# A token-major second MLP product, attention scores from rounded halves, and queries projected in smaller parts

## The reference

```python
s = jnp.einsum('bqhgd,bkhd->bhgqk', q_blk, k, preferred_element_type=jnp.float32) * (HEAD_DIM ** -0.5)
p = jax.nn.softmax(s, axis=-1).astype(v.dtype)
...
x = x + gt1[..., None, :] * branch_merge(attn_x, gla_x, ga, gg, w_br_attn, w_br_gla, w_out)
x = x + gt2[..., None, :] * sq_relu_mlp(modulate(rms_norm_2(x, norm2), sh2, sc2), w_mlp1, w_mlp2)
...
def sq_relu_mlp(h, w1, w2):
    return jnp.square(jax.nn.relu(h @ w1)) @ w2
```

## Time and profile before

| what | value |
|---|---|
| median of three runs | 1803.73 us (1802.23 to 1803.89) |
| the profiled execution, its own time | 1801.4 us |
| its span, from first to last recorded instruction | 1799.6 us |
| TensorE busy | 1737.3 us, 97% of the span |
| VectorE, ScalarE, GpSimd busy | 1020.6, 802.6, 725.2 us |
| granted TensorE clock, mean | 0.998 of full speed |
| HBM traffic | 84 GB/s over the span |

### The profile page before, as it was taken

How to read it: one execution, slowest core, us unless ns; L and a number is a source line. 1 busy time by engine, 2 the same in 40 slices (tenths; PEclk the granted TensorE clock), 3 DMA queues, 4 the chain that set the end, 5 groups by cost and what they waited for, 6 DMA issues and landing times.

```text
span 1799.6 us, 25063 instructions
## 1 busy us (share of the span) xinstructions
PE 1737.3 (97%) x9011; PEld 1399.6 (78%) x9011; DVE 1020.6 (57%) x1560; ACT 802.6 (45%) x1364; POOL 725.2 (40%) x795
## 2 busy tenths in 40 slices
PE   8999999998999899999999999999999999999998
PEld 6777777776777567778878888888888878888887
DVE  6688786677647874456649838766733331212122
ACT  4445454466546664345552254564533342313231
POOL 3645545443543104321114432233244545555563
PEclk9999999999999999999999999999999999999999
DMA  6342422221222001211018721112123323333332
GB/s 209 91 121 89 126 85 82 71 69 37 76 92 76 20 17 50 71 43 29 24 56 277 232 68 42 42 47 59 47 83 94 105 71 101 99 94 93 104 95 94
DMA packets 238798, 152.11 MB, mean 85 GB/s; under 512 B 7997, under 2 KB 223046, under 8 KB 238694
## 3 DMA queue, kind: packets, MB, share of 16 engines
q1 hardware_dynamic: 225758, 125.50, 24.1%
q10 hardware_dynamic: 12936, 25.21, 4.1%
HBM read 148.59 MB, written 2.10 MB: 84 GB/s over the span
## 4 chain that ended last, share of the span: by engine, by line
PE 65%; issue 11%; DVE 8%; POOL 7%; ACT 7%; DMA 1%; POOLq 0%; DVEq 0%; ACTq 0%; SPq 0%
PE ps L657 17%; PE ps L661 17%; PE ps L658 16%; POOL wl L607 7%; PE ps L2176 2%; PE ps L2158 1%; PE ps L1614 1%; PE ps L1646 1%; ACT wh L620 1%; PE ps L2165 1%; PE ps L2645 1%; PE ps L2679 1%; DVE pairs L2917 1%; PE ps L2159 1%; DVE queries L1917 1%
## 5 line engine op out<-in xcount | busy, mean ns | idle before, releaser
L607 POOL TENSOR_TENSOR wl<-raw,wh 128x256 fp32r<-128x256 f32 (+1 forms) x775 | 701.7, 937 | 1014.3 <-ACT wh L620 1014.3
L657 PE MATMUL ps<-ah,wh 128*128 128x512 f32 (+1 forms) x1144 | 461.8, 404 | 12.5 <-ACT gate_u L2718 4.2
L661 PE MATMUL ps<-ah,wl 128*128 128x512 f32 (+1 forms) x1144 | 447.6, 391 | 0.3
L658 PE MATMUL ps<-al,wh 128*128 128x512 f32 (+1 forms) x1144 | 446.3, 390 | 0.0
L620 ACT ACTIVATE wh<-raw 128x1024 fp32r<-128x1024 f32 (+1 forms) x220 | 230.6, 1049 | 305.2 <-PE ps L661 293.3
L657 PEld LDWEIGHTS ps<-ah,wh 128*128 128x128 f32 (+1 forms) x1144 | 214.0, 187 | 68.0 <-issue 11.1
L661 PEld LDWEIGHTS ps<-ah,wl 128*128 128x128 f32 (+1 forms) x1144 | 213.7, 187 | 49.9 <-POOL wl L607 2.1
L658 PEld LDWEIGHTS ps<-al,wh 128*128 128x128 f32 (+1 forms) x1144 | 214.3, 187 | 44.2 <-issue 1.4
L657 PE MATMUL ps<-bh,wh 128*128 128x512 f32 (+1 forms) x588 | 232.8, 396 | 5.7 <-DVE resid L1471 2.6
L661 PE MATMUL ps<-bh,wl 128*128 128x512 f32 (+1 forms) x588 | 230.0, 391 | 1.5 <-POOL wl L607 1.4
L658 PE MATMUL ps<-bl,wh 128*128 128x512 f32 (+1 forms) x588 | 229.1, 390 | 0.0
(11 more groups left out here) (434 smaller groups left out, 2729.2 us busy)
## 6 DMA issues: line engine op xcount, KB each, us to landing
raw<-w_mlp SPq DMA_DIRECT2D x64, 512.0 KB, 3.8
raw<-w_in SPq DMA_DIRECT2D x52, 512.0 KB, 3.7
raw<-ssm_w_in SPq DMA_DIRECT2D x40, 512.0 KB, 3.8
ada_late<-w_ada ACTq DMA_DIRECT2D x16, 1024.0 KB, 6.7
ada_raw<-w_ada ACTq DMA_DIRECT2D x16, 512.0 KB, 3.8
raw<-ssm_w_out SPq DMA_DIRECT2D x16, 512.0 KB, 3.3
raw<-mla_w_in SPq DMA_DIRECT2D x11, 512.0 KB, 3.7
raw<-mla_w_out SPq DMA_DIRECT2D x8, 512.0 KB, 3.5
```

What stands on the lines that cost most here:

```text
L607: nc.gpsimd.tensor_tensor(wl[:, s, part], raw[:, s, part], wh[:, s, part].bitcast(F32), ALU.subtract).then_inc(lo_ready, LOW_PIECES * (par ...
L657: nc.tensor.matmul(dst, w_hi[k], x_hi[k], start=k == 0, stop=False)
L658: nc.tensor.matmul(dst, w_hi[k], x_lo[k], start=False, stop=False)
L661: ins = nc.tensor.matmul(dst, w_lo[k], x_hi[k], start=False, stop=k == n - 1)
```

## The change

Six things at once.

1. The second MLP product is token-major: hidden activations are stationary (128 tokens), 512 columns of the weights move, and 4 token tiles by 2 column halves go to 8 PSUM banks. Each half's results are multiplied by the gate, laid out as rows (`gate_rows`), and added to `o_tok`, which starts as the transposed `resid`. The transposes, 8 groups of 4, move to the front of the MLP; the gate rows are made by 8 matmuls of `ones` by a diagonal matrix. Results are stored in 8 parts instead of 4.
2. The scores of the grouped-query attention are made of three fp32r matmuls of high and low halves, for which ScalarE and VectorE split queries and keys. The key head 1 is scaled later, projections of queries keep a distance of two heads, the sum of squares moves from t = 1 to t = 0.
3. The query projection of the latent attention is spread over all four heads of a quad: 9, 6, 6 and 6 matmuls.
4. The two `modulation` calls are put apart, before units 8 and 9.
5. `stay_busy(2, 9)` before the first scores of the latent attention is new; in front of the MLP `stay_busy(3, 10)` and `stay_busy(3, 16)` become `stay_busy(1, 10)`.
6. ScalarE's second and third `take_q` of a quad come one head later (`Q_TAKEN`).

```diff
-                if g < CTX_BLOCKS // 2:
-                    modulation(2 * g)
-                    modulation(2 * g + 1)
                 for n in range(8, 10):
+                    if g < CTX_BLOCKS // 2:
+                        modulation(2 * g + n - 8)
                     projection("ssm", g, n)
...
             project_q(0, 1)
+            stay_busy(2, 9)
             scores(0)
...
-                if h // QUAD + 1 < QUADS and h % QUAD < 3:
-                    project_q(h // QUAD + 1, h % QUAD)
+                if h // QUAD + 1 < QUADS:
+                    for piece, ks in Q_PARTS[h % QUAD]:
+                        project_q(h // QUAD + 1, piece, ks)
...
+        Q_PARTS = (((0, (0, 1, 2)),), ((1, (0, 1)),), ((1, (2,)), (2, (0,))), ((2, (1, 2)),))
+        Q_TAKEN = (0, None, 1, 2)
...
-                nc.tensor.matmul(bank(b), q, k_feat[:, j // QPK, 0:T], start=True, stop=True)
-                nc.tensor.matmul(bank(b + 1)[:, 0:CTX], q, k_feat[:, j // QPK, T:TA], start=True, stop=True).then_inc(sem("g_scores"), 1)
+                terms = ((q_hi, k_hi), (q_hi, k_lo), (q_lo, k_hi))
+                for cols, dst in ((slice(0, T), bank(b)), (slice(T, TA), bank(b + 1)[:, 0:CTX])):
+                    for k, (q, keys_) in enumerate(terms):
+                        ins_ = nc.tensor.matmul(dst, q[:, j % 2, tile], keys_[:, j // QPK, cols], start=k == 0, stop=k == 2)
...
+            def high_q(j):
+                nc.scalar.activation(q_hi[:, j % 2], p_cos[:], ACT.Copy).then_inc(sem("qk_high"), 1)
+            def low_q(j):
+                nc.vector.tensor_tensor(q_lo[:, j % 2], p_cos[:], q_hi[:, j % 2].bitcast(F32), ALU.subtract).then_inc(sem("qk_low"), 1)
...
-            stay_busy(3, 10)
+            for c in range(DC):
+                ins_ = nc.tensor.matmul(bank(2 + c // 4)[:, c % 4 * P:(c % 4 + 1) * P], ones[:], gate_diag[:, c], start=True, stop=True)
+            for k in range(3):
+                turn_resid(k)
             norm_pe_summed(pe, "norm2", norm_v[:, 1])
-            stay_busy(3, 16)
+            turn_resid(3)
+            turn_resid(4)
+            stay_busy(1, 10)
...
+            def token_major(i, half, q):
+                last = q == DC // OUT_KS - 1
+                for k, t in ([(k, t) for t in range(TT) for k in range(OUT_KS)] if last else [(k, t) for k in range(OUT_KS) for t in range(TT)]):
+                    c, tok, dst = q * OUT_KS + k, slice(t * P, (t + 1) * P), bank(OUT_BANKS[half][t])
+                    nc.tensor.matmul(dst, bh[:, c, tok], vh[:, k], start=c == 0, stop=False)
+                    nc.tensor.matmul(dst, bl[:, c, tok], vh[:, k], start=False, stop=False)
+                    low(k, T)
+                    ins_ = nc.tensor.matmul(dst, bh[:, c, tok], vl[:, k], start=False, stop=c == DC - 1)
...
-                for c in range(DC):
-                    nc.vector.scalar_tensor_tensor(resid[:, c], bank(c % 2), mod[:, 5 * DC + c, 0:1], resid[:, c], ALU.mult,
-                                                   ALU.add).then_inc(acc_free[c % 2], 1)
+                for k in range(2 * TT):
+                    part = nc.vector.tensor_tensor(out_part[k % 2], bank(b), gate_rows[:, cols], ALU.mult)
+                    nc.vector.tensor_tensor(o_tok[:, t, cols], o_tok[:, t, cols], out_part[k % 2], ALU.add).then_inc(sem("out_copied"), 1)
```

More of the change, by code:

```diff
@@ L51 @@
 LATE_COLS = 16
+OUT_KS = 2
 K_UNIT = KVH + 1
@@ L1800, in act_mla @@
                     exp(h + 1, 3)
-                if h // QUAD + 1 < QUADS and h % QUAD < 3:
-                    take_q(h // QUAD + 1, h % QUAD)
+                if h // QUAD + 1 < QUADS and Q_TAKEN[h % QUAD] is not None:
+                    take_q(h // QUAD + 1, Q_TAKEN[h % QUAD])
                 if h % 2 and h > 2:
@@ L2029, in _build @@
         p_sin = r("p_sin", [P, T])
-        q_feat = r("q_feat", [P, 2, T])
+        q_hi, q_lo = r("q_hi", [P, 2, T], F32R), at("q_lo", [P, 2, T], F32R, gos_at)
+        k_hi, k_lo = (at(f"k_{n}", [P, KVH, TA], F32R, ARENA_END + k * KVH * TA * 4) for k, n in enumerate(("hi", "lo")))
         probs_at = r.at
@@ L3066, in block @@
                     done_1.then_inc(unit_done, 1)
[L3067 removed]
+                for n in range(2 if first else 0, DC):
+                    if first and 4 <= n < 7:
+                        if n > 4:
+                            pe.wait_ge(sem("out_copied"), n - 3)
+                        turn_resid(n + 1)
                     low = unit_high(pe, "mlp", i, n)
                     pe.wait_ge(acc_free[n % 2], i * per_bank + (ACC0["mlp"][n % 2] + 1 + n // 2))
[L3070 to L3085 removed]
+                    project(bank(n % 2), "mlp", n, chunk(ah), chunk(al), DC, P, low=low).then_inc(unit_done, 1)
+                for half in range(2):
+                    if first:
+                        pe.wait_ge(sem("out_copied"), 9)
+                    else:
+                        pe.wait_ge(sem("o_free"), i * 6 + (0 if half else -2))
+                    if half:
+                        for b in range(2):
+                            pe.wait_ge(acc_free[b], i * per_bank + (ACC0["mlp"][b] + 1 + 4))
+                    for q in range(DC // OUT_KS):
+                        token_major(i, half, q)
+            mlp_blocks(pe, block)
         def mlp_blocks(eng, block):
@@ L3156, in block @@
                         nc.vector.tensor_tensor(bl[:, n - 1], norm_v[:, (n - 1) % 2], bh[:, n - 1].bitcast(F32), ALU.subtract).then_inc(sem("hid_low"), 1)
-                for c in range(DC):
-                    dve.wait_ge(unit_done, i * 16 + (unit("mlp", 0, DC + c) + 1 + CREDIT))
-                    nc.vector.scalar_tensor_tensor(resid[:, c], bank(c % 2), mod[:, 5 * DC + c, 0:1], resid[:, c], ALU.mult,
-                                                   ALU.add).then_inc(acc_free[c % 2], 1)
+                    if isinstance(i, int) and i == 0:
+                        for k in COPIES.get(n, ()):
+                            copy_resid(k)
```

187 lines of the change are left out of this document (119 added, 68 removed).

## The result

The changed kernel took 1791.96 us in the median of 5 runs (1790.9 to 1792.09), the kernel before 1803.73 (1799.67 to 1804.69): ratio 0.993, 95% interval 0.9918 to 0.9941. The gain is 11.8 us, where 17.8 had been forecast; 1792 is inside the range and is the figure of the first rival, for reasons that are not quite its own. Against each other the two profiled executions stand 10.5 us apart (spans 1799.6 and 1789.1).

A forecast was written before the change was run, and what follows sets the result against it. TensorE, busy 97% of the span, was taken as the bound. Gains of 6.2 (grouped-query), 3.9 (end), 3.5 (latent attention), 2.9 (clock) and 1.3 (modulation) sum to 17.8: from 1803.7 to 1786, range 1780 to 1794.

The forecast's parts named there:

- the first rival: Latent attention: softmax chain of 5.5 us holds TensorE, fills find no idle time, clock drops stay; 1792, chance 0.17.
- A tile's 0.24: Grouped-query scores: six matmuls take 1.05 instead of 1.29 us, gaining 0.24 in each of 28 tiles, 6.7.
- The end: Behind the last matmul: 5.6 gained; 1.3 lost in the first MLP trip, 0.35 ahead of the MLP; net 3.9.
- The latent attention: Spread query projection fills idle time in fourth-head passes, 3.5 gained; first scores at full clock, 1.3.
- No wait in the token-major units: Second MLP product: rival of late low weight pieces in 32 units, slower than before, 1805 at 0.6 each; chance 0.03.
- two rivals: Latent fills and clock gain nothing, 1792, chance 0.17; grouped-query stage bound by the query split, 1793, chance 0.10.
- The term for the unit behind the modulation: Mamba: eight narrow matmuls before the last projection give GpSimd's split time; 1.0 gained in group 0, 0.3 in group 1.
- The clock term: Half-clock windows go: 1.6 gained in Mamba around 257 us, 1.3 at the latent attention's first scores; 2.9 together.
- The entry: Start of the grouped-query stage: counted as zero, between a gain of 1.5 and a loss of 3.
- The slack for the low half: Grouped-query heads: query's low half ready at about 4.8 of 5.1 us; 0.5 taken off for lateness.

The follow-up runs named there:

- modulation apart: The kernel before with only a projection put between the two halves of a group's modulation sums; 1803.38 us, ratio 0.9993 to the kernel before.
- the changed kernel again: The changed kernel, unedited, run on another chip beside the kernel before; 1790.78 us, ratio 0.9933 to the kernel before.

## Why the prediction was right and where it was not

**Right in mechanism and size.** A tile's 0.24 (0.25 measured). The end: 5.9 for 5.6 (with two errors in it that cancel in part, a later VectorE and a shorter store), 1.5 for 1.3 in the MLP and 0.3 for 0.35 ahead of it. The latent attention: 4.4 for 4.8, of which the full clock gave 1.7 (1.3 forecast) and the filled passes 2.7 (3.5). No wait in the token-major units. The first rival gave the right time for wrong reasons: the fills did find idle time. That 1792 lies in the range is in part luck: the high end of 1794 was put there for two rivals, and neither came true.

**The term for the unit behind the modulation failed (1.3 forecast, 0 measured).** The step was "give the split that much more time". It took a wait's releaser, GpSimd, and asked when TensorE's previous unit ended; the chain in front of GpSimd is ScalarE's, whose split stands behind copies and silus in a written order. The last matmul of the earlier unit was not what ended last. The modulation sums only moved, from before one unit to before the next.

**The clock term failed in Mamba (1.6 forecast, 0 measured)** by the same wait. The window did go, but what it costs is only what TensorE would otherwise have gained, and here the wait for low pieces stood behind it. Two runs show it from both sides: without the window nothing gained, with a window in group 0 nothing lost. In the latent attention no such wait stands behind the first pass, and there the clock's term was right.

**The grouped-query stage's ends were mis-sized.** The entry was taken as 0, between a gain of 1.5 and a loss of 3; it lost 1.9. (The first scores start 3.4 later in the stage, but 2.0 of that is nine projection matmuls that now stand ahead of them. At the seventh tile's scores the stage is 1.2 behind in time and one sum of squares, 0.9, ahead in work: 0.4 lost net, where six tiles' own gain is 1.5.) It was read as a sum of operations; part of it is the order of ScalarE's queue, where a copy stands behind another unit's split while VectorE waits: two lines in another order gave 1.6 back. The end of the stage, from the 27th tile on, was counted at nothing and lost 1.4. The slack for the low half was enough in the steady heads; for the last, no projection lengthens the passes ahead of it, and TensorE waits 1.7. The prediction had looked at that head for its own scores alone. 6.6 from 26 tiles, less 1.9 and 1.4, are 3.3; measured 3.4.

**Left out altogether:** that windows of half clock also turn up in one execution and not in another. The two places that the prediction priced did recur: each of the four profiles of kernels that keep the 32 narrow matmuls in a row has a window behind them, each of the four that keep the empty wait ahead of the first scores has one there, and of the ten with the change none has either (table below). The others, such as 1207 and 21 us, come and go, and the prediction had no term for them. Over the runs of the kernel before, its time and its mean clock go together: 1799.43 us at 0.999, around 1804.5 at 0.996 to 0.997, 1807.56 at 0.995, and the profiled execution with two windows shows 0.998. The changed kernel's runs have 0.997 to 0.999 and spread over 1.2 us on one chip and 0.7 on another. The least disturbed executions, with the clock at 1.000, are 1799.45 (modulation apart, which gains nothing) and 1789.23 (transposes in place of idle products), 10.2 apart, and the parts in the traces without the clock add up to the same (3.4 + 2.7 + 4.2 = 10.3). The runs of both kernels at 0.999 stand 8.4 to 9.3 apart. So I put 9 to 10 us of the gain to work and waits and some 2 to fewer windows; this division rests on comparing runs of several kernels, and no run measured it by itself.

## What to carry to other kernels

Before a wait is priced, follow its releaser's own queue backwards: time that TensorE saves ahead of a wait whose end is set by another engine's written order is given back in full, and so is a window of low clock there. A new operation between two engines should be walked through at the stage's entry and in its last repetition, where the filler that hides it is missing. A window of half clock in one profile may recur in every execution or be a draw among the weak places of the program: look at the same place in profiles of several kernels before it is given a price, and ask how many such places a change removes.

## What the chip showed that I had not expected

- Windows of half clock last 3.4 us each. The fourteen profiles, one of each kernel, have them here (those behind TensorE's last instruction, where nothing is left to slow down, are left out):

| place, us | just ahead of it | profiles with a window there |
|---|---|---|
| 154 or 257 | 32 narrow matmuls in a row | 4 of 4; with the modulation apart 0 of 10 |
| 566 to 568 | a wait of 2.4 | 4 of 4; with idle products in it 0 of 10 |
| 600 or 601 | a wait of 2.65 | 2 of 4; with the query projection spread 0 of 10 |
| 21 | a wait of 1.3 | 6 of 14 |
| 1136 to 1154, 1204 to 1213 | a wait of 1.23 | 6 of 11, one of them twice; with idle products in it 0 of 3 |
| 404, 414, 908 | waits of 1.3, 2.1, 2.2 | 1 each |
| 1038 | a row of narrow matmuls | 1 |

  Identical work around 1138 and 1205 us was hit in some executions and not in others. The Trainium skill says in "TensorE: Matmul & The Clock Gate", section "Part 1: The HAM clock gate", that the gate's window runs freely and does not start with the kernel; the two runs of the changed kernel, with the window at 1207 in one and at 21 in the other, agree.
- A window's cost depends on what stands behind it: 1.6 us at 1207, 1.1 at 21 (the changed kernel again), 0 at 154 and 257.
- An idle product of fp32 128 x 128 is two records and takes 0.24 us, a transpose is one and takes 0.12 (20 records in 2.45 and 2.35).
